# A hybrid decoder step on Trainium2: value pages issued by ScalarE, scalings moved from VectorE to ScalarE, and another spread of the key steps

## What is computed

```python
def even_mixer(h, pos, s0, k_past, v_past, ...):
    proj = h @ w_in                                   # 1024 -> 4608 columns
    rq, rk, rv, rg, dq, dk, dv = jnp.split(proj, EVEN_SPLITS, axis=-1)
    rq, rk = rope(rq, pos), rope(rk, pos)
    ro, s_fin = retention(rq, rk, rv, s0)             # per head: decays gamma**(i+1), gamma**-(i+1), state times gamma**128
    ro = head_group_norm(ro) * jax.nn.silu(rg)        # minus mean, by the root of the variance
    dq, dk = rope(rms_norm(dq, qg), pos), rope(rms_norm(dk, kg), pos)
    do = diff_attn(dq, [k_past, dk], [v_past, dv], ...)   # (softmax(q1 k1) - lam softmax(q2 k2)) v
    do = rms_norm(do, sub_g) * (1.0 - lam_init)
    return concat([ro, do]) @ w_out, ...
```

## Time and profile before

| | us |
|---|---|
| median of 3 runs | 2200.06 |
| lowest and highest | 2194.59, 2203.4 |
| the profiled execution: time | 2195.29 |
| the profiled execution: span of its core | 2193.5 |
| busy: TensorE, VectorE, ScalarE, GpSimd | 1888.4, 996.0, 540.3, 635.1 |
| mean granted TensorE clock, as a share | 0.909 |

### The profile page before, as it was taken

How to read it: one execution, slowest core, us unless ns; L and a number is a source line. 1 busy time by engine, 2 the same in 40 slices (tenths; PEclk the granted TensorE clock), 3 DMA queues, 4 the chain that set the end, 5 groups by cost and what they waited for, 6 DMA issues and landing times.

```text
span 2193.5 us, 35957 instructions
## 1 busy us (share of the span) xinstructions
PE 1888.4 (86%) x14217; PEld 1713.2 (78%) x14217; DVE 996.0 (45%) x1400; ACT 540.3 (25%) x822; POOL 635.1 (29%) x519
## 2 busy tenths in 40 slices
PE   5855778666756687999999999997999999999998
PEld 5753545444544446999999999987999999999998
DVE  2696676954654434443234333338332344323421
ACT  4321122221111202322122223330322323212211
POOL 1366352554565300133023110002311413301400
PEclk8976767878777888999999999997999999999999
DMA  7144664677877772232223222220232322323231
GB/s 225 60 149 146 206 210 155 207 252 244 270 244 258 246 250 97 87 96 87 96 87 96 94 92 77 75 68 14 74 100 87 96 92 83 101 92 89 86 104 59
DMA packets 218304, 288.05 MB, mean 131 GB/s; under 512 B 12993, under 2 KB 149778, under 8 KB 217890
## 3 DMA queue, kind: packets, MB, share of 16 engines
q1 hardware_dynamic: 215306, 281.95, 39.7%
q0 software_dynamic: 656, 1.51, 0.4%
q10 hardware_dynamic: 2208, 2.75, 0.4%
HBM read 274.96 MB, written 11.21 MB: 130 GB/s over the span
## 4 chain that ended last, share of the span: by engine, by line
PE 68%; DVE 11%; issue 7%; DMA 5%; SPq 3%; POOL 3%; ACT 2%; ACTq 0%; DVEq 0%; POOLq 0%
PE ps L1604 17%; PE ps L1606 17%; PE ps L1605 16%; PE ps L1425 4%; PE ps L1427 4%; PE ps L1426 4%; DMA vbuf<-in_cache_v 3%; POOL kbuf L636 3%; DVE Sc L1112 2%; SPq L498 2%; PE ps L1460 2%; DMA kbuf<-in_cache_k 1%; SPq L497 1%; PE ps L1671 1%; DVE w_lo L487 1%
## 5 line engine op out<-in xcount | busy, mean ns | idle before, releaser
L487 DVE TENSOR_TENSOR w_lo<-raw,w_hi 128x1024 fp32r<-128x1024 f32 x238 | 335.7, 1418 | 509.0 <-ACT w_hi L480 507.7
L636 POOL TENSOR_TENSOR kbuf<-kbuf,Qb 128x512 f32<-128x512 f32 x256 | 338.5, 1349 | 217.5 <-DMA kbuf<-in_cache_k 161.0
L1604 PE MATMUL ps<-xg_hi,w_hi 128*128 128x260 f32 x1408 | 399.6, 284 | 0.5 <-DVE sTs L1380 0.5
L1606 PE MATMUL ps<-xg_hi,w_lo 128*128 128x260 f32 x1408 | 399.4, 284 | 0.0
L1605 PE MATMUL ps<-xg_lo,w_hi 128*128 128x260 f32 x1408 | 398.2, 283 | 0.0
L1425 PE MATMUL ps<-w_hi,xg_hi 128*128 128x256 f32 (+1 forms) x1200 | 370.6, 309 | 14.8 <-DVE w_lo L487 6.4
L480 ACT ACTIVATE w_hi<-raw 128x1024 fp32r<-128x1024 f32 x248 | 258.7, 1052 | 458.3 <-PE ps L1606 411.3
L1426 PE MATMUL ps<-w_lo,xg_hi 128*128 128x256 f32 (+1 forms) x1200 | 360.8, 301 | 0.0
L1427 PE MATMUL ps<-w_hi,xg_lo 128*128 128x256 f32 (+1 forms) x1200 | 359.5, 300 | 0.0
L1604 PE MATMUL ps<-h_hi,w_hi 128*128 128x260 f32 x1024 | 289.7, 283 | 0.0
L1606 PE MATMUL ps<-h_hi,w_lo 128*128 128x260 f32 x1024 | 289.6, 283 | 0.0
(11 more groups left out here) (266 smaller groups left out, 2579.7 us busy)
## 6 DMA issues: line engine op xcount, KB each, us to landing
kbuf<-in_cache_k SPq DMA_DIRECT2D x256, 256.0 KB, 3.8
vbuf<-in_cache_v SPq DMA_DIRECT2D x256, 256.0 KB, 3.4
raw<-in_w_ffn_up SPq DMA_DIRECT2D x64, 512.0 KB, 3.9
raw<-in_w_ffn_down SPq DMA_DIRECT2D x64, 512.0 KB, 3.4
raw<-in_w_in_odd SPq DMA_DIRECT2D x48, 512.0 KB, 3.8
raw<-in_w_in_even SPq DMA_DIRECT2D x36, 512.0 KB, 5.4
raw<-in_w_out_odd SPq DMA_DIRECT2D x24, 512.0 KB, 3.4
raw<-in_w_out_even SPq DMA_DIRECT2D x12, 512.0 KB, 3.4
```

The source lines that it names most:

```text
L487: dve.tensor_tensor(w_lo[:, c.slot], raw[:, c.slot % 2], w_hi[:, c.slot].bitcast(F32), ALU.subtract).then_inc(lo_made, 1)
L636: pool.tensor_tensor(kk, kk, Qb[:, s % 2, :], ALU.mult).then_inc(k_weighed, 1)
L1604: pe.matmul(out, wh, xh, start=kk == 0, stop=False, skip_group_check=True)
L1606: mm_ = pe.matmul(out, wl, xh, start=False, stop=kk == KC * groups - 1, skip_group_check=True)
```

## The change

- The value pages are issued by ScalarE, in halves of two pages (`VL`, quad, half), and SP issues keys alone. Half 0 of quad n + 1 stands behind V step n, half 1 with the next key step, two pages each. The first two quads are issued by ScalarE ahead of the first evacuation, the second behind the wait for xT to be saved.
- The key steps are two a slot from macro 4 on (the fifth), and `snew` moves from slot (5, 2) to (5, 0).
- The decays go into the scale of the evacuation of macros 6 to 9 (a table `dcy`, two activations for one), and ScalarE copies `rkn` behind the transposes.
- In the attention, both maxima are taken by one instruction, the division by the first sum moves to ScalarE's copy of the output, and VectorE mixes with one ratio.
- In the retention, the state is updated by one instruction, ScalarE copies the output (`rB`) and applies the normalisation (`rC`) with a scale and a bias; VectorE keeps the statistics and the gate.

```diff
@@ kv_step
     n, part = divmod(PER * (j - LAG), QUAD)
-    if 0 <= n < NQ and part == 0:
-        out.append(("V", n))
+    if 0 <= n < NQ:
+        if part == 0:
+            out.append(("V", n))
+        if n > 0:
+            out.append(("VL", n - 1 + Q_SLOTS, part // PER))
@@ plan
-    after[5, 2].append(("snew",))
+    after[5, 0].append(("snew",))
...
-                if step < STEPS and (n == 0 or m > 4):
+                if step < STEPS and (n == 0 or m > 3):
                     after[m, t] += kv_step(step)
@@ values_in
-        def values_in(eng, n):
+        def values_in(eng, n, half):
...
-                for j in range(QUAD):
+                for j in range(PER * half, PER * half + PER):
                     page(eng, vbuf[n % Q_SLOTS][:, j, :], cache_v, QUAD * n + j, v_loaded[n % Q_SLOTS])
@@ SP
-            for n in range(LOW_QUADS):
-                values_in(sp, n)
...
-            for n in range(LOW_QUADS, Q_SLOTS):
-                values_in(sp, n)
...
-                        if step[0] == "V" and step[1] > 0:
-                            values_in(sp, step[1] - 1 + Q_SLOTS)
@@ ScalarE, evacuate
-                act.activation(dst, src, func, scale=rstdN[rows, t:t + 1]).then_inc(nat_read, 1)
+                if m in ROPED[4:]:
+                    for hh in range(2):
+                        at = slice(DKR * hh, DKR * hh + DKR)
+                        h = 2 * (m % 2) + hh
+                        last = act.activation(dst[:, at], src[:, at], func, scale=dcy[rows, (m - 6) // 2, t, h:h + 1])
+                    last.then_inc(nat_read, 1)
+                else:
+                    act.activation(dst, src, func, scale=rstdN[rows, t:t + 1]).then_inc(nat_read, 1)
@@ ScalarE, steps
+                    if i >= 8:
+                        h = 2 * (i % 2) + hh
+                        act.activation(rkn[:, :, DKR * h:DKR * h + DKR], stg[:, ROPED.index(i) % 3, 0:NT, DKR * hh:DKR * hh + DKR],
+                                       ACT.Copy, scale=GAMMA[h] ** P).then_inc(rkn_made, 1)
...
+                elif kind == "VL":
+                    values_in(act, i, step[2])
...
-                    act.activation(doN[:, q, P * h:P * h + P], ps[:, OUT, 0:P], ACT.Copy).then_inc(out_read, 1)
+                    act.activation(doN[:, q, P * h:P * h + P], ps[:, OUT, 0:P], ACT.Copy, scale=rzu[:, 2 * i:2 * i + 1]
+                                   ).then_inc(out_read, 1)
...
+                elif kind == "rB":
+                    h, n = step[1:]
+                    act.wait_ge(out_ready, OUT_FILL[step] + 1)
+                    if h == 0 and n == 0:
+                        act.wait_ge(v_stored, 16)
+                    act.activation(ro[:, n, DVR * h:DVR * h + DVR], ps[:, OUT, 0:DVR], ACT.Copy).then_inc(out_read, 1)
+                elif kind == "rC":
+                    h, n = step[1:]
+                    act.wait_ge(r_biased, h + 1)
+                    out = ro[:, n, DVR * h:DVR * h + DVR]
+                    act.activation(out, out, ACT.Identity, scale=rs4[:, n:n + 1], bias=nb4[:, n:n + 1]).then_inc(r_normed, 1)
...
             act.wait_ge(rstd_made, 1)
+            act.wait_ge(pt_loaded, 16)
+            for n in range(LOW_QUADS):
+                for half in range(QUAD // PER):
+                    values_in(act, n, half)
+            act.wait_ge(x_saved, 16)
+            act.wait_ge(xg_lo_made, KD)
+            for n in range(LOW_QUADS, Q_SLOTS):
+                for half in range(QUAD // PER):
+                    values_in(act, n, half)
@@ VectorE, rot_step
-                chain(dve.tensor_tensor(x3, x3, dec.unsqueeze(2).broadcast_to([P, 2, DKR]), ALU.mult))
...
-                if m >= 8 and t < NT:
-                    dve.tensor_copy(rkn[:, t, cols], x)
@@ VectorE, dA and dE
-                    for m in range(2):
-                        last = dve.tensor_reduce(mxm[:, m:m + 1], ps[:, PAIR[m], 0:nk], AXX, ALU.max)
-                    chain(last)
+                    chain(dve.tensor_reduce(mxm, ps[:, PAIR[0]:PAIR[0] + 2, 0:nk], AXX, ALU.max))
...
-                    chain(dve.tensor_tensor(rz[:, 1:2], rz[:, 1:2], nlam, ALU.mult))
-                    chain(dve.tensor_scalar(pq[:, 0, 0:nk], pq[:, 0, 0:nk], rz[:, 0:1], None, ALU.mult))
-                    dve.scalar_tensor_tensor(pq[:, 0, 0:nk], pq[:, 1, 0:nk], rz[:, 1:2], pq[:, 0, 0:nk], ALU.mult, ALU.add
+                    chain(dve.scalar_tensor_tensor(ratio, rz[:, 1:2], nlam, zz[:, 0:1], ALU.mult, ALU.mult))
+                    dve.scalar_tensor_tensor(pq[:, 0, 0:nk], pq[:, 1, 0:nk], ratio, pq[:, 0, 0:nk], ALU.mult, ALU.add
@@ VectorE, rA, rB and rC
-                        chain(dve.tensor_tensor(new, ps[:, PAIR[1], 0:DVR], old, ALU.add))
-                        dve.tensor_scalar(new, new, g128, None, ALU.mult).then_inc(r_state, 1)
+                        dve.scalar_tensor_tensor(new, old, GAMMA[h] ** P, ps[:, PAIR[1], 0:DVR], ALU.mult, ALU.add
+                                                 ).then_inc(r_state, 1)
...
-                    dve.wait_ge(out_ready, OUT_FILL[step] + 1)
-                    dve.tensor_copy(out, ps[:, OUT, 0:DVR]).then_inc(out_read, 1)
...
-                    chain(dve.tensor_scalar(out, out, mv4[:, 2 * n:2 * n + 1], rs4[:, n:n + 1], ALU.subtract, ALU.mult))
+                    dve.wait_ge(r_normed, NT * h + n + 1)
@@ PE, rA
+                    if n == 0:
+                        pe.wait_ge(rkn_made, h + 1)
```

## The result

| | before | after |
|---|---|---|
| median, us | 2201.7 (4 runs) | 2437.9 (4 runs) |
| lowest and highest | 2194.6, 2203.4 | 2425.9, 2439.9 |
| span of the profiled execution | 2193.5 | 2438.1 |
| mean granted TensorE clock | 0.909 | 0.87 |

The changed kernel is slower: ratio 1.107, 95% interval 1.102 to 1.111. The forecast was 2400 us in a range of 2270 to 2490.

What follows compares the result with a forecast made beforehand. The prediction took the first stage to be bound by waits around a loop, value pages queued behind key pages on SP. Its terms 165+8+28+7-3 gave +205 on 2195.3 us: 2400 us, range 2270 to 2490.

Steps and rivals of the forecast that it cites:

- The new loop: First stage: tile end, evacuation, two page issues, landing, V step, next tile; each slot closes on itself, half a slot ahead.
- Retention slots: 39 first-stage slots with retention: 11.75 us each plus softmaxes and table loads, 501 against 336 us, +165 (+95 to +230).
- Moved work ahead of the issue: Retention copy or normalisation on ScalarE between evacuation and page issue: mean 0.4 us a slot, bounds 0.2 and 0.8.
- Landing: Time for a value page to arrive after issue: 3.4 us taken, 2.8 to 4.2; the skill's formula gives 2.6.
- Attention slots: 20 first-stage slots with differential attention: 12.0 us each plus three softmaxes of 6, 258 against 250 us, +8 (-20 to +50).
- Start: Start of the V stream: three slots now lie behind V step 0, +28 us (20 to 34).
- prologue: Before the first evacuation: both first quads issued by ScalarE ahead of it, moving it to 47.8 us, +7 (0 to +10).
- Tail: End of the first stage: one V step there instead of four, -3 us (-15 to +5).
- VectorE's relief: Work moved off VectorE in the first stage gains nothing, as VectorE is not in the loop; otherwise up to -20 us.
- Rival 3: ScalarE pays more per page than SP or waits for activations to drain, 0.8 us or more a slot: 2450 to 2520; chance 0.05.
- Rival 2: Value pages freed from SP's queue remove TensorE's page waits and the loop does not bind: 2147 us; chance 0.08.
- Rival 1: Waits short enough for the fast clock level, pages landing in 2.6 us: +62, 2257 us; chance 0.06.

Runs made afterwards that it cites:

- e1: Changed kernel with ScalarE issuing all four pages of the next quad behind the V step, instead of two of them one key step later: 2219.0 us.
- e9: Kernel before plus value pages issued by ScalarE in halves and the new key-step spread, without the moves from VectorE to ScalarE: 2401.2 us.
- e4: Changed kernel with value pages back on SP and key steps as before, leaving only the moves from VectorE to ScalarE: 2197.0 us, ratio 0.998.
- e3: Kernel before with value pages issued by ScalarE in halves and nothing else of the change: 2173.1 us, ratio 0.988.
- e12: e2 with one edit, the softmax's second step (subtraction, exponentials) placed first in its slot: 2136.6 us, ratio 0.971.
- e2: Changed kernel with key steps as before: single through macro 4, snew in slot (5, 2): 2173.2 us, ratio 0.988.
- e10: e2 with the softmax's second step first in its slot and the first two value quads issued two pages a slot behind macro 0: 2126.0 us.
- e6: e2 with the first eight value pages issued behind macro 0 instead of ahead of the first evacuation: 2171.3 us.

## Why the prediction held, and where it did not

The direction and the mechanism were right, and so was the place of most of the loss. That the total lies within 38 us of the forecast is in part luck: the attention slots and the tail missed by 46 and 13 us one way and the retention slots by 20 the other. The terms of its sum:

- **The new loop** was right and is shown: undoing it alone (e1) took back 219 of 236 us, and 53 waits and 309.9 us of them are the "over 50 waits and 200 us". The transfer rate fell to 164 GB/s (foretold about 180) and the clock fell.
- **Retention slots**, 501 foretold and 480.7 measured, inside the bounds. The 35 slots in which no softmax ends were 11.57 us, where the sum had 11.75 and 0.33 for table loads. Part by part: V step and tile 6.08 (6.15 in the sum), evacuation 0.51 (0.6), from there to the last page's issue 1.67 (0.4 and 1.2, and the table loads), landing of that page 3.26 (3.4), and 0.06 to the V step. The softmaxes came to 30 us as foretold, but by two errors against each other: the sum had five of 6 us. There were four in this stretch; the intervals of three were 20.1, 22.2 and 21.4 us, 8.5 to 10.6 more than an ordinary slot, and that of the last, behind the last keys, was 12.1.
- **Moved work ahead of the issue** was somewhat low: 0.4 us a slot in the sum, bounds 0.2 and 0.8, and 0.60 by the difference of after and e9. I had priced the instructions. What costs is mostly that ScalarE's normalisation waits for VectorE's statistics, and these for a weight split. The moves also slowed the V step and tile by 0.38, which the sum did not have.
- **Landing**: the formula quoted from the Trainium skill (DMA: Bandwidth & Descriptors, Anatomy of one DMA — SWDGE (gpsimd) path) is a fit for transfers issued by GpSimd. Value pages are issued by SP and ScalarE here, so the formula was not made for them, though the least row came close to it. The measured landings after were 2.5 at the least, 3.3 at the median and 8.0 at the most.
- **Attention slots** were mis-sized, and outside their bounds: +54 for +8. The step that failed is "three softmaxes of 6". They cost 26.7, 25.3 and 32.1 less 12.9, that is 13.8, 12.4 and 19.2. I had counted keys ahead of the subtraction, from a retention slot, and left out the rotation and the mixing that stand in the same queue in an attention slot. The ordinary slot was 12.9, not 12.0. Together 45.4 - 18 and 20 x 0.93 come to the 46 us missed.
- **Start** +29.0 for +28, and **prologue** +9.3 for +7. ScalarE's first evacuation stood behind eight pages, as foretold, at 50.1 us and not 47.8. The sum had the second quad wait for the saving of xT, until 44.4. The trace shows no such wait: the first page went out at 43.55, behind ScalarE's own work, and all eight were in the way.

```profile
43.55 6.54 ACTq L504 DMA_DIRECT2D vbuf<-in_cache_v  x8
50.14 0.84 ACT L791 ACTIVATE stg<-ps,small 128x256 f32<-128x256 f32 x2 [7.22 <-issue]
```

- **Tail** had the wrong sign, +9.7 for -3, inside its bounds. TensorE there, in order of time:

```profile
1016.50 1.17 PE L1489 MATMUL ps<-vbuf,Pe 128*8 128x512 f32 x8 [4.01 <-DMA vbuf<-in_cache_v]
...
1027.69 1.90 PE L1489 MATMUL ps<-vbuf,Pe 128*8 128x512 f32 x8 [9.07 <-DMA vbuf<-in_cache_v]
1029.51 3.78 PE L1514 MATMUL ps<-srv,kmask 8*128 8x256 f32 x8
...
1041.63 1.99 PE L1514 MATMUL ps<-srv,kmask 8*128 8x256 f32 x8
...
1070.51 3.78 PE L1514 MATMUL ps<-srv,kmask 8*128 8x256 f32 x8
```

  The last V step waited 9.1 us with all state steps behind it, and most of these then ran at 3.78 us for eight matmuls where 1.99 shows in between; the granted clock from 1016 to 1072 us was 0.60, nearer the 1.2 GHz level than the 2.4 GHz one, where it was 0.81 in the tail before. I had counted V steps and not the clock of the matmuls behind them. e9 has the same V steps in its tail and took 51.7 us at a clock of 0.73, 2.2 under the kernel before and close to the forecast. What made the clock of the tail lower with the moves stays open.
- **VectorE's relief** at nothing: e4 shows it, net of the work that ScalarE took over.
- **Rival 3** (a page costs ScalarE more than SP, or waits for activations to drain) falls: from one page to the next are 0.82 us, the same step as on SP, and at 669.97 us a page went out while the normalisation of 0.60 us begun at 669.53 still ran. **Rival 2** was right in its mechanism (e3) and wrong for this spread. **Rival 1** fell on its fast level: pages landed in 2.8 us in the slots above and in 3.26 on the mean, from tile end to V step passed 3.9 to 8.3 us, and V step and tile took 6.08 us and not 3.9. Its price was off too: the attention slot of 10.8 us should be 11.15 by its own terms, which makes its +62 some +69.

## What to carry to other kernels

A transfer's lead is set by the last of its pieces and by the step that the issuing engine must get through first: when an issue moves to a computing engine, count how many tiles stand between the issue and the use for every piece, since a reordering with the same amount of work can take that number from one to zero. Parts measured alone can add up to +12 us and cost +236 together. And before a reduction is called slow, look at what stands ahead of its reader in the reader's queue: putting one subtraction first in its slot was worth 1.7% (e12 against e2).

## What the runs showed of the hardware

- **A cross-partition reduction on GpSimd is ready at once; GpSimd is not.** `PARTITION_ALL_REDUCE` took 0.40 us and VectorE read its result 0.03 us after it ended (e10 above), but GpSimd's next multiply came 7.4 us later. In all 14 kernels, seven softmaxes each, that pause was 6.7 to 10.9 us. The Trainium skill (GPSIMD Engine Reference, Instruction dispatch) tells of a load of about 6 us at the first call to a freshly loaded kernel, without an instruction in the profile. The gap is of that size; no run here isolates its cause.
- **VectorE slows under GpSimd's multiplies.** In the softmax of the changed kernel the same two instructions took 0.22 and 0.35 us at 262 us, with GpSimd idle, and 0.90 and 1.32 us at 282 us, under a run of eleven key multiplies of 1.29 us. The Trainium skill (SBUF — State Buffer, Who interferes with whom) says that a VectorE instruction with two SBUF inputs contends with a GpSimd instruction that reads SBUF, and that such contention is an exclusive lock. The trace agrees: from 276.85 us on the rotation and the mixing took 1.23 to 1.37 us an instruction (the 128x1 one 0.90), about one multiply, and the same 128x128 step of the rotation ran at 0.29 us in GpSimd's pause in e10. There it is about four times cheaper.
- **Issuing a page costs an engine's queue 0.82 us** on ScalarE as on SP. An activation begun ahead of the issue runs on beside it (669.53 us above), but one that stands behind waits: eight pages in a row took 6.5 to 6.7 us, and the evacuation behind them was held up for 7.2 us in the changed kernel and 6.2 in e6.
